# Splitting the residual load in two and converting half of the branch input under the last gate tile, in a fused decoder layer on one core

## The reference

```python
xn = rmsnorm(x, p["norm_mix_g"])
aq, ak, av, dq, dk, dvv, dz, da, db, ga, gb = split_cols(xn @ p["w_in"], IN_SPLITS)
...
ya = swa_prompt(aq, ak, av, p["sinks"])                       # 512 wide
...
o, new_S = gated_delta(qh, kh, heads(dvv), g, beta, dn_state, chunk)
yb = (rmsnorm(o, p["dn_norm_g"]) * silu(heads(dz))).reshape(B, L, DN_WIDTH)   # 512 wide
mix = sigmoid(ga) * (ya @ p["w_br_a"]) + sigmoid(gb) * (yb @ p["w_br_b"])
h = x + mix @ p["w_mix_out"]
hq = rmsnorm(h, p["norm_x_g"]) @ p["w_xq"]                    # then cross-attention, then a conv MLP
mk, mv = split(rmsnorm(mem, norm_mem_g) @ w_xkv)              # keys and values of 256 memory rows
```

## Time and profile before

| | us |
|---|---|
| median of three runs | 2052.7 (2052.44 to 2054.99) |
| the profiled execution, its own time | 2047.56 |
| the profiled execution, its span | 2045.8 |
| PE busy in the span | 1893.3 (93%) |
| DVE, ACT, POOL busy | 978.7, 481.5, 663.8 |
| mean granted PE clock | 0.987 of full speed |

### The profile page before, as it was taken

One profiled execution on the slowest core, in us unless ns is written; L12 is line 12 of the kernel. 1 busy time (PEld: TensorE's weight loads), 2 busy tenths in 40 slices (PEclk: granted clock), 3 DMA queues, 4 the chain that ended last, 5 costly groups with the idle time before them and its releaser, 6 DMA issues.

```text
span 2045.8 us, 31783 instructions
## 1 busy us (share of the span) xinstructions
PE 1893.3 (93%) x13257; PEld 1781.5 (87%) x13257; DVE 978.7 (48%) x1141; ACT 481.5 (24%) x897; POOL 663.8 (32%) x334
## 2 busy tenths in 40 slices
PE   3988899999898898998999799999999999999997
PEld 2976799987777787897988679999999999999996
DVE  6367466754554232355132527634544454345356
ACT  4145326642222103412121623100000000000012
POOL 2321033310100112344673014533434344343335
PEclk8999999999999999999999999999999999999998
DMA  4211111110102021313122211111111111111112
GB/s 182 76 46 42 38 42 32 40 63 23 36 26 63 24 78 69 135 52 126 63 73 75 100 73 45 42 52 41 49 43 41 51 41 42 50 41 51 41 45 85
DMA packets 45467, 119.71 MB, mean 59 GB/s; under 512 B 3793, under 2 KB 20881, under 8 KB 44209
## 3 DMA queue, kind: packets, MB, share of 16 engines
q1 hardware_dynamic: 45376, 118.39, 17.3%
HBM read 102.94 MB, written 15.77 MB: 58 GB/s over the span
## 4 chain that ended last, share of the span: by engine, by line
PE 67%; DVE 7%; ACT 3%; issue 2%; DMA 1%; DVEq 0%; POOL 0%; SPq 0%; ACTq 0%
PE PS L531 41%; PE PS L1892 11%; PE PS L1299 3%; PE PS L1497 2%; PE PS L1919 1%; PE PS L1535 1%; PE PS L1775 1%; PE PS L1692 1%; ACT TMP L1161 1%; DMA RAW<-in_w 1%; DVE H L2527 1%; PE PS L1839 1%; PE PS L1860 1%; DVE XL L511 1%; PE PS L1582 0%
## 5 line engine op out<-in xcount | busy, mean ns | idle before, releaser
L736 POOL TENSOR_TENSOR WH<-RAW,CST 128x1024 fp32r<-128x1024 f32 x118 | 230.3, 1951 | 1292.1 <-PE PS L531 729.3
L531 PE MATMUL PS<-XH,WH 128*128 128x352 f32 x2280 | 504.3, 329 | 32.0 <-DVE XL L492 9.9
L531 PE MATMUL PS<-XH,WL 128*128 128x352 f32 x2280 | 494.1, 324 | 0.0
L531 PE MATMUL PS<-XL,WH 128*128 128x352 f32 x2280 | 493.7, 325 | 0.0
L531 PEld LDWEIGHTS PS<-XH,WH 128*128 128x128 f32 x2280 | 389.9, 190 | 48.5 <-issue 27.4
L531 PEld LDWEIGHTS PS<-XH,WL 128*128 128x128 f32 x2280 | 393.8, 189 | 0.0
L531 PEld LDWEIGHTS PS<-XL,WH 128*128 128x128 f32 x2280 | 389.9, 189 | 0.0
L738 POOL TENSOR_TENSOR WL<-RAW,WH 128x1024 fp32r<-128x1024 f32 x118 | 317.0, 2687 | 9.3
L2492 DVE TENSOR_TENSOR H<-H,PS 128x1056 f32<-128x1056 f32 x80 | 100.2, 1254 | 131.8 <-PE PS L1892 131.8
L1892 PE MATMUL PS<-AH,WH 128*128 128x352 f32 x480 | 104.3, 326 | 1.9 <-DVE H L2492 1.9
L1892 PE MATMUL PS<-AL,WH 128*128 128x352 f32 x480 | 104.6, 326 | 0.0
(11 more groups left out here) (440 smaller groups left out, 2426.3 us busy)
## 6 DMA issues: line engine op xcount, KB each, us to landing
RAW<-in_w SPq DMA_DIRECT2D x136, 512.0 KB, 3.5
H<-in_xT SPq DMA_DIRECT2D x4, 1056.0 KB, 8.3
TMP<-in_xT SPq DMA_DIRECT2D x1, 4224.0 KB, 14.1
early_gates<-DV SPq DMA_DIRECT2D x18, 176.0 KB, 2.0
out_yT<-H SPq DMA_DIRECT2D x4, 704.0 KB
early_gates<-A SPq DMA_DIRECT2D x12, 176.0 KB, 1.8
DV<-early_gates SPq DMA_DIRECT2D x1, 2112.0 KB, 14.0
TMP<-early_gates SPq DMA_DIRECT2D x2, 1056.0 KB, 6.8
```

Source lines behind the costliest of these rows:

```text
L531: mm = nc.tensor.matmul(PS[:, 3 * mm_g + c, 0:CW], w_[:, p, off + k * P:off + (k + 1) * P], x_[:, xk0 + k, c * CW:(c + 1) * CW], start=fir ...
L736: nc.gpsimd.tensor_tensor(WH[:, p, :], RAW[:, p, :], one, ALU.mult).then_inc(w_hi, 1)
```

## The change

Four edits. On PE the last gate tile is written out, and its 36th matmul of 72 (the end of k step 3, after which XH and XL tiles 0 to 3 are not read any more) raises gate_mm. On ACT the four copies into XH that come from YA stand ahead of the last sigmoid and wait for gate_mm; the four from H stay behind it. On SP the residual input is loaded in two transfers of 128x4x1056: the first after four branch tiles are finished, between the loads of slots 43 and 44, the second after all eight, with the loads of slots 44 to 48 ahead of it and 49 behind it. On DVE residual(0) waits for the first transfer only, and residual(4) for the second.

```diff
-            loads(42, 48)
+            loads(42, 44)
+            sp.wait_ge(br_s, 4)
+            sp.dma_start(x_res[:, 0:4, :], d["xT"][0:4].rearrange("k p t -> p k t")).then_inc(xres_in, 16)
+            loads(44, 48)
+            loads(48, 49)
             sp.wait_ge(br_s, 8)
-            sp.dma_start(x_res, d["xT"].rearrange("k p t -> p k t")).then_inc(xres_in, 16)
-            loads(48, 66)
+            sp.wait_ge(xres_in, 16)
+            sp.dma_start(x_res[:, 4:8, :], d["xT"][4:8].rearrange("k p t -> p k t")).then_inc(xres_in, 16)
+            loads(49, 50)
+            loads(50, 66)
...
-                pairs(act, n, gate)
+                for t in range(n):
+                    gate(t, (t0 + t) % 2)
             act.wait_ge(out_done, n_dn_state)
-            gates(0, GC, lambda t: H[:, 4 + t, :])
-            act.wait_ge(z_y, 4)
-
             def split_heads(src, base, tiles=range(KT)):
                 for k in tiles:
                     nc.scalar.activation(XH[:, k, :], src(k), ACT.Copy).then_inc(y_hi, 1)
-            split_heads(lambda k: YA[:, k, :] if k < 4 else H[:, k - 4, :], 0)
+            gates(0, GC - 1, lambda t: H[:, 4 + t, :])
+            heads_src = lambda k: YA[:, k, :] if k < 4 else H[:, k - 4, :]
+            act.wait_ge(gate_mm, 2 * (GA + GB) + 1)
+            split_heads(heads_src, 0, range(0, 4))
+            gates(GC - 1, 1, lambda t: H[:, 4 + GC - 1 + t, :])
+            act.wait_ge(z_y, 4)
+            split_heads(heads_src, 0, range(4, KT))
...
-            for t in range(2, GC):
+            for t in range(2, GC - 1):
                 gate_tile(t, t % 2)
+            t = GC - 1
+            pe.wait_ge(w_split, SLOTS["gate"][0] + t + 1)
+            pe.wait_ge(acc_free, acc0["gate"] + t - 1)
+            for k in range(KT):
+                mm = gemm_part(1 - t % 2, t % 2, k, KT)
+                if k == KT // 2 - 1:
+                    mm.then_inc(gate_mm, 1)
+            mm.then_inc(w_used, 1)
...
-            dve.wait_ge(xres_in, 16)
-
             def residual(t, p):
+                if t % 4 == 0:
+                    dve.wait_ge(xres_in, 16 + 4 * t)
```

## The result

| | before | changed |
|---|---|---|
| median of four runs, us | 2052.57 (2050.9 to 2054.99) | 2036.71 (2032.43 to 2044.14) |
| ratio, 95% interval | | 0.9927 (0.9904 to 0.9949) |
| profiled execution, span, us | 2045.8 | 2042.3 |
| mean granted PE clock in it | 0.987 | 0.984 |

The medians differ by 15.9 us; 11.7 were forecast. The ratio puts the difference at 15.0 us, with an interval from 10.5 to 19.7, in which the forecast 11.7 lies. One run of all that follow, among those of "POOL waits for rests", took 2384.2 us at a granted clock of 0.749 and is left out of its median and ratio. The two profiled spans differ by only 3.5 us, so something else moves these times, and the traces have to be compared piece by piece.

A forecast was written before the change was run, and what follows sets the result against it. PE is busy for 93% of the span, so time can only be won where it stands still or runs below full clock. 6.2 + 6.4 - 0.9 = 11.7 us off the 2052.7 median gave 2041.0 us, range 2038 to 2047.

The forecast's parts named there:

- A: Last gate sigmoid to end of branch tile 0: of 7.5 us lost, 6.2 won, a 1.23 us stop left.
- B: End of branch tile 7 to end of mix tile 1: 6.4 us won, 0.9 lost again to DVE beside POOL.
- the 2 us by which the runs differ: Whole kernel: allowance for run spread, part of the range's 14.7 us won end.
- more than 13 us: Whole kernel: case of a larger gain, from waits further on that also shorten; chance 0.03.
- the same work in any run: Both lost stretches: same in any run, so the 11.7 us gain was taken off the median 2052.7.
- the 0.9 us taken as free: Mix tile 0: last XL subtraction ends at 951.2, PE wants it at 952.1, so 0.9 us were free.
- 1.4 for this term: Mix tile 0: by the shared-port rule, POOL's 1.04 + 1.26 us block DVE, less the free 0.9; total gain 11.2.
- the two ends: Branch stage, first residual half: slot 44's load lands at 899.6 (cheap) or 904.5 us (dear), costing PE nothing either way.
- The point from which PE notices: Branch stage: slot 44 costs PE nothing until it lands after 906.7, 15.4 us after SP's wait ends.
- Rival (c): Branch stage: SP's new wait at br_s 4 starves POOL, kernel slower, 2057 us or more; chance 0.03.
- (a): Only one of the two gaps closes: 5 to 8 us won, about 2046.5 us; chance 0.16.
- (b): Nothing is won, waits go to the next in line at both places: 2052.7 us, within 0.2%; chance 0.08.

The follow-up runs named there:

- POOL waits for rests: Changed kernel plus a wait: POOL begins slot 48 only when DVE has made all eight rests of the mix input; 2043.63 us, ratio 0.9936.
- seven repeated ones: The changed kernel timed again without any edit, with more rounds; 2040.43 us, ratio 0.9942 against the kernel before.
- exchanged banks: Changed kernel with the branch stage's two PSUM bank groups exchanged, so only branch tile 0's second half needs the last sigmoid; 2042.75 us, ratio 0.9928.
- wait one tile later: Changed kernel with SP's first wait for five finished branch tiles instead of four; 2048.53 us, ratio 0.9974.
- both additions: Changed kernel with both POOL's wait for all eight rests and the exchanged PSUM bank groups; 2035.99 us, ratio 0.9917.

## Why the prediction came out as it did

**The spread of the runs failed, and with it the range.** The mechanism was right, and so was the size of the gain: 11.7 us forecast, 11.2 us in A and B, 11.0 us between two executions with the same start. The base was right too: 2052.7 was forecast from, and the kernel before measured 2052.57. The step that failed is the term of the range for "the 2 us by which the runs differ". Three runs from 2052.44 to 2054.99 looked like a narrow distribution. Thirty on one chip went from 2046.17 to 2059.13, 13 us, and the eleven runs of the changed kernel from 2032.43 to 2044.14. Three of its first four runs were below 2037, at a mean granted clock of 0.989 to 0.991 where the fourth had 0.984, and the median of the four is 3.7 us below that of the seven repeated ones, 2040.43. That this second median is 0.6 us from the forecast 2041.0 is luck as well, for beside it the kernel before has 2055.05. There was a sign of the spread before: the profiled execution's 2047.56 lay 5 us below three runs that agreed within 2.6 us. I noted the distance and did not ask what it says about the spread. By its number the result fell into the case of more than 13 us, "from waits further on that also shorten", which had 0.03; no trace shows such waits.

The prediction also took the lost time as "the same work in any run". It is not quite that: with the same code A lost 7.5 us in one execution and 6.4 in another, and B 6.4 and 7.6. That the sum was hit within 1 us owes something to the execution that was profiled.

**A was right.** 6.09 us instead of 6.2; the stop left is 1.14 us for 1.23, the clock stays up behind it, ACT's four copies and DVE's four subtractions took 4.01 and 4.76 us as in the rows, the second four subtractions the slow 6.98. That only the last sigmoid's bank keeps PE waiting is shown by the exchanged banks. One reason given for the clock was no reason: that the first three matmuls took 0.72 us "like every first three after a stop". At 840.82 and 961.30 they took 1.25, and at 926.31 they took 0.72 with a clock of 0.66 behind the earlier trace rows.

**B was right in its cause and 0.4 us off in its loss.** Lost time of 6.42 us before, 5.10 won, so 1.32 went to DVE's subtractions beside POOL; 0.9 was forecast. POOL's wait gives 1.36 back. The delay itself was priced well: four subtractions took 7.78 instead of 5.85 us, 1.93 more, and two hits of 0.9 from one row made 1.8. What was too large is the 0.9 us taken as free, which was counted for the last subtraction; PE's last stop, at 955.75, is on the one before it (the last ends at 949.09 + 7.78 = 956.87), and of the 1.93 us only 0.6 were free. The Trainium skill's rule (SBUF — State Buffer, section "SBUF: two separate sides"), by which the loser is blocked for the other's whole instruction, gave 1.4 for this term. The traces agree with the rule in kind: the second and third of the four subtractions, beside POOL, took 4.34 us together where they took 2.41 in the kernel before, and all four are back at 5.85 where POOL is kept out. The 1.4 came out close by two errors that cancel, 1.04 + 1.26 = 2.3 us of blocking for 1.93 and 0.9 us free for 0.6.

**The residual halves.** The transfer was issued at 895.1, and slot 44's split began at 905.63, 10.5 us later, between the two ends (8.3 and 13.2); 2.0 us after branch tile 4's end, where within 1 us of it was forecast. PE noticed nothing: branch tiles 1 to 7 take 86.54 us for 86.53. The point from which PE notices was put at 15.4 us; with the wait one tile later the transfer was issued at 907.16, the split began 9.1 us behind it and about 20 us behind the old wait, and PE stopped for 4.87 us, which puts the point at about 15. Rival (c) names a real cost that this change stays short of by some 5 us. Of rivals (a) and (b) there is no sign: neither place has a stop above 1.4 us that it did not have before.

**What stays open.** Why one execution runs the delta-rule stage at full clock and the next, of the same code, does not. No run here steers it, and none was made to; so whether the change shifts the odds stays open as well.

## What to carry to other kernels

When the profiled execution and the timed runs of the same kernel disagree by more than the gain in question, cut the traces at fixed marks and compare stretches; medians of a few runs then carry whatever happened elsewhere, and a forecast's range has to carry it too. In an in-order load queue look at what stands behind a big transfer rather than at the transfer: moving one small weight load ahead of it was worth as much here as cutting the transfer in two and starting it early. When a wait is taken away, price the work that now starts earlier by what it collides with: POOL's split, free to start, held DVE up by 1.9 us and cost PE 1.4, and one more wait gave that back.

## What the runs showed of the hardware

I had not expected the clock to go with 13 us of a single-core kernel's time. Of the thirty runs of the kernel before, the nine under 2049 us show a mean granted clock of 0.987 to 0.989, the seven over 2057 one of 0.981 or 0.982. The clock fell after stops that it survived elsewhere: the same stop of 2.78 us in branch tile 7 was followed by a granted clock of 0.66 over five us in the changed kernel, and by full clock with the banks exchanged, where the branch tiles then took 84.97 instead of 86.54 us. It is not the exchange that does it: with both additions, which has the same exchange, the clock behind that stop was 0.67 and the tiles took 86.53. Busy time by stretch, PE alone, from just before that stop's end; first the changed kernel:

```profile
core 0: us, PE busy (x), PEclk, DMA share, GB/s
929.80:934.80 5.00, 4.74 (x20) 0.66 0.26 75
```

and with the banks exchanged:

```profile
929.50:934.50 5.00, 4.78 (x30) 1.00 0.29 81
```

In the first 20 matmuls ran, part of the time at 1.2 GHz, in the second 30, all at 2.4 GHz. So a row on one stop says what the clock did there once, not what it does after every stop of that length.
